# One decoder step: x loaded and turned ahead of the modulation, query rows spread through device memory

## The reference

```python
mod = (silu(c) @ ada_w + ada_b)                      # c: 1 + 8 rows; ada_w: 1024 x 6144
sh1, sc1, g1, sh2, sc2, g2 = split(mod, 6)
h = rms_norm(x, norm1_w) * (1 + sc1) + sh1
proj = h @ w_in                                      # pooling, attention q k v, delta rule, gates
q_a, k_a = rms_norm(q_a), rms_norm(k_a)              # per head of 64
y = concat(pool_mixer, moba_attention, gated_delta_rule)
x = x + g1 * (y @ w_out)
h2 = rms_norm(x, norm2_w) * (1 + sc2) + sh2
x = x + g2 * ((silu(h2 @ w_gate) * (h2 @ w_up)) @ w_down)
```

## Time and profile before

| what | value |
|---|---|
| median of 3 runs | 603.79 us (603.11 to 609.97) |
| the profiled execution: its time, its span | 604.71 us, 603.0 us |
| mean granted TensorE clock | 0.952 of full |
| PE busy, PEld busy | 541.0 us (90%), 445.9 us (74%) |
| DVE, ACT, POOL busy | 347.3 us (58%), 168.2 us (28%), 44.2 us (7%) |
| DMA | 114.68 MB, mean 190 GB/s |

### The profile page before, as it was taken

The page is one execution under the profiler, slowest core; times in us unless marked ns, Lnnn a source line. Parts: engine busy times, 40 slices in busy tenths (PEclk is TensorE's granted clock), DMA queues, the critical chain, the costliest instruction groups (busy, mean ns, idle before and its releaser), DMA issues.

```text
span 603.0 us, 10197 instructions
## 1 busy us (share of the span) xinstructions
PE 541.0 (90%) x3917; PEld 445.9 (74%) x3917; DVE 347.3 (58%) x541; ACT 168.2 (28%) x235; POOL 44.2 (7%) x107
## 2 busy tenths in 40 slices
PE   4759999998899898988879789987999999999997
PEld 2428678576578776667554139876999999999996
DVE  1046276658688897956655536475565466454441
ACT  2310110632122223321000215253433434334331
POOL 7300000000102910000011000000000000000000
PEclk9888989989689999999989889997999999999999
DMA  5997338356129485725639998594546645545201
GB/s 196 304 344 241 91 120 279 117 127 221 60 70 302 140 264 167 253 78 203 208 90 386 365 359 290 161 289 156 181 152 198 197 153 191 171 162 192 72 20 37
DMA packets 99437, 114.68 MB, mean 190 GB/s; under 512 B 7343, under 2 KB 82240, under 8 KB 99372
## 3 DMA queue, kind: packets, MB, share of 16 engines
q1 hardware_dynamic: 93368, 104.46, 54.2%
q10 hardware_dynamic: 5188, 7.67, 3.8%
q0 software_dynamic: 832, 1.89, 0.8%
HBM read 111.20 MB, written 2.97 MB: 189 GB/s over the span
## 4 chain that ended last, share of the span: by engine, by line
PE 69%; DVE 16%; DMA 6%; ACT 4%; issue 3%; ACTq 1%; SPq 1%; DVEq 0%
PE bank L335 65%; DVE prod L917 3%; DVE s_all L1013 3%; DMA ring<-in_ada_w_dram 2%; DVE mats L917 2%; DMA ring<-in_w_out_dram 2%; DMA ring<-in_cache_v_dram 1%; DVE cv L1121 1%; DVE BTP L917 1%; PE bank L387 1%; PE bank L358 1%; ACT w_part L1704 1%; DMA prod<-in_dn_norm_w_dram 1%; ACT adaS L1536 1%; PE bank L518 1%
## 5 line engine op out<-in xcount | busy, mean ns | idle before, releaser
L335 PE MATMUL bank<-a_hi,w_part 128*128 128x264 f32 x832 | 154.5, 287 | 2.1 <-DVE a_lo L1458 2.1
L917 DVE TENSOR_TENSOR w_part<-ring,w_part 128x2048 fp32r<-128x2048 f32 (+1 forms) x38 | 84.9, 2236 | 90.8 <-ACT w_part L1704 90.8
L335 PEld LDWEIGHTS bank<-a_hi,w_part 128*128 128x128 f32 x832 | 130.8, 191 | 2.6 <-issue 2.6
L335 PE MATMUL bank<-a_lo,w_part 128*128 128x264 f32 x416 | 119.0, 286 | 0.0
L1704 ACT ACTIVATE w_part<-ring 128x2048 fp32r<-128x2048 f32 (+1 forms) x38 | 70.9, 1869 | 86.8 <-PE bank L335 75.4
L335 PE MATMUL bank<-hT,ring 128*128 128x264 f32 x352 | 87.4, 411 | 4.1 <-ACT proj L1559 2.1
L335 PEld LDWEIGHTS bank<-hT,ring 128*128 128x128 f32 x352 | 71.0, 204 | 20.2 <-issue 7.4
L335 PEld LDWEIGHTS bank<-a_lo,w_part 128*128 128x128 f32 x416 | 79.6, 191 | 0.1
L335 PE MATMUL bank<-hid_hi,w_part 128*128 128x264 f32 x352 | 64.9, 285 | 0.0
L335 PEld LDWEIGHTS bank<-hid_hi,w_part 128*128 128x128 f32 x352 | 54.6, 188 | 0.1
L335 PE MATMUL bank<-hid_lo,w_part 128*128 128x264 f32 x176 | 49.7, 283 | 0.0
(11 more groups left out here) (321 smaller groups left out, 569.6 us busy)
## 6 DMA issues: line engine op xcount, KB each, us to landing
ring<-in_ada_w_dram SPq DMA_DIRECT2D x24, 1024.0 KB, 7.1
ring<-in_cache_k_dram SPq DMA_DIRECT2D x64, 256.0 KB, 3.6
ring<-in_w_in_dram SPq DMA_DIRECT2D x11, 1024.0 KB, 6.0
ring<-in_w_gate_dram SPq DMA_DIRECT2D x11, 1024.0 KB, 5.3
ring<-in_w_up_dram SPq DMA_DIRECT2D x11, 1024.0 KB, 5.3
ring<-in_cache_v_dram SPq DMA_DIRECT2D x40, 256.0 KB, 4.1
ring<-in_w_down_dram SPq DMA_DIRECT2D x8, 1024.0 KB, 5.3
ring<-in_cache_v_dram ACTq DMA_DIRECT2D x24, 256.0 KB, 4.8
```

The costliest lines, as they stand in the source:

```text
L335: return pe.matmul(out, lhsT, rhs, start=start, stop=stop, skip_group_check=True)
L917: return v.tensor_tensor(out, a, b_, op)
```

## The change

In the first stage:
- SP issues the two loads of c and then goes straight to the ring. The eleven small loads into `rows` go to ACT's queue behind the loads of x, the page table to POOL's; SP waits for the table only ahead of the first K item.
- ACT's nine later small loads go to POOL's queue, behind the masks; the count row is made ahead of the masks, and VectorE's work on it stands at the very start and behind the copies of x.
- TensorE begins with eight `keep_awake` matmuls, then turns x, then c, then the rows, then adds up the mean square (chunk by chunk), and only then begins with the modulation. All copies out of the turns are VectorE's, the squares are ACT's, one chunk at a time.
- Groups 0 and 1 are multiplied one behind the other (banks 2 and 3); each turn comes a group later than its multiplication, and there are more `keep_awake` matmuls between. The first four chunks of `hT` are scaled when group 2 is reduced, the others when group 3 is.

In the attention of the decoding sequences `QB` is dropped from TensorE and ACT. POOL stores the eight query rows to a buffer in device memory and reads each row back with a transfer that writes it to all 128 partitions; the transfers of queries 2 to 7 wait until the half of `qb` is free and stand at chosen places of POOL's order.

```diff
@@ tensor
+            pe.wait_ge(sem("ident_made"), 1)
+            keep_awake(7, 8)
+            pe.wait_ge(sem("x_in"), 16 * (TT + 1))
+            for c in range(DC):
+                b = opened(f"xT{c}", 4 + c % 4)
...
+            pe.wait_ge(sem("c_silu"), 1)
+            b = opened("cT", 0)
...
+            pe.wait_ge(sem("rows_in"), 16 * 11)
+            b = opened("rowsT", 1)
...
+            b = opened("ss1", 6)
+            for c in range(DC):
+                pe.wait_ge(sem("sq1"), c + 1)
+                last = mm(b[:, 0:NT], ones[:, :], hT[:, c, :], c == 0, c == DC - 1)
+            closed(last, "ss1")
             pe.wait_ge(sem("cT_made"), 1)
-            for j in range(2 * D // IW // 2):
-                ada(j)
-                ada_turn(j)
-                if j == 1:
-                    square_sums("ss1", "sq1", hT)
+            ada(0, 2)
+            ada(1, 3)
+            ada_turn(0, 0)
+            ada(2, 2)
+            ada_turn(1, 1)
+            keep_awake(0, 4)
+            ada(3, 3, 2)
+            ada_turn(2, 0)
+            keep_awake(1, 3)
+            ada_turn(3, 1)
+            keep_awake(0, 8)
@@ vector
+            def norm_half(c0, c1):
+                modulation(1, R_N1, c0, c1)
+                norm_rows(0, c0, c1)
+                for c in range(c0, c1):
+                    inc(v.tensor_scalar(hT[:, c, 0:T], hT[:, c, 0:T], scA[:, c, 0:1], modT[:, c, 0:1], ALU.mult, ALU.add),
+                        "h1")
+            mod_reduce(0)
+            mod_reduce(1)
+            mod_reduce(2)
+            norm_half(0, DC // 2)
+            mod_reduce(3)
+            norm_half(DC // 2, DC)
@@ k_item
-                v.wait_ge(sem("qb"), q + 1)
+                v.wait_ge(sem(f"qb{q % 2}"), 16 * (q // 2 + 1))
@@ gpsimd
+            def spread_query(q):
+                if q >= 2:
+                    g.wait_ge(sem("k_scored"), q - 1)
+                g.dma_start(qb[:, q % 2, :], q_dram[q, :].partition_broadcast(P)).then_inc(sem(f"qb{q % 2}"), 16)
+            g.wait_ge(sem("q_rows8"), 1)
+            g.dma_start(q_dram[:, :], nat8[:, 0, :]).then_inc(sem("q_stored"), 16)
+            g.wait_ge(sem("q_stored"), 16)
+            for q in range(4):
+                spread_query(q)
             g.wait_ge(sem("ebc"), 1)
...
+            spread_query(4)
             g.wait_ge(sem("k_rows"), 2)
...
+            spread_query(5)
             g.wait_ge(sem("proj_out"), out_count(PCH - 1))
...
+            spread_query(6)
             g.wait_ge(sem("tails"), 3)
...
+            spread_query(7)
             g.wait_ge(sem("max_diag"), 1)
@@ sync
             cols = {"ada": ada_w, "win": w_in, "wout": w_out, "gate": w_gate, "up": w_up}
-            sp.wait_ge(sem("table_in"), 16)
             for it in stream:
                 kind, i = it
+                if it == ("k", (0, 0)):
+                    sp.wait_ge(sem("table_in"), 16)
```

More of the change, by code:

```diff
@@ L228, in build @@
         hidden = sb("hidden_f", [P, 2, NT])
+        q_dram = nc.dram_tensor("q_rows_dram", [NS, AW], F32, kind="Internal").ap()
         bank = [ctx.enter_context(nc.psum_tensor(f"bank{i}", [P, 512], F32)) for i in range(8)]
@@ L342, in keep_awake, with ada @@
                     mm(bank[b][:, 0:P], ident[:, :], ident[:, :])
[L345 to L361, removed]
+            def ada(j, b_=3, awake=0):
                 opened(f"ada{j}", b_)
                 for n in range(2):
+                    keep_awake(1, awake)
                     last = ada_half(j, n)
@@ L441, in to_rows8 @@
                 closed(last, name)
[L443 to L447, removed]
             def kv_rows(name, c0, ready, n):
@@ L928, in _ @@
             step(v.memset(st4[:, :, :], 0.0))
-            b = full(v, "rowsT")
-            step(v.tensor_copy(constT[:, 0:NR], b[:, 0:NR]))
-            v.sem_inc(bank_free[2], 1)
+            v.wait_ge(sem("iota_made"), 1)
+            for c in range(PCH):
+                for g in range(2):
+                    r = slice(64 * g, 64 * g + 64)
+                    step(v.tensor_scalar(rcnt[r, c, :], rcnt[r, c, :], float(WINDOWS[2 * c + g]), None, ALU.min))
+            for c in range(DC):
+                b = full(v, f"xT{c}")
+                freed(v.tensor_copy(xT[:, c, :], b[:, 0:NT]), f"xT{c}")
             b = full(v, "cT")
             freed(v.tensor_copy(cT[:, :, 0:NC], b[:, 0:DC * NC].rearrange("p (c r) -> p c r", c=DC)), "cT")
-            v.wait_ge(bank_free[3], frees_at("cT"))
+            v.wait_ge(bank_free[0], frees_at("cT"))
             v.sem_inc(sem("cT_made"), 1)
-            for c in range(0, DC, 2):
-                b = full(v, f"xT{c}")
-                freed(v.tensor_copy(xT[:, c, :], b[:, 0:NT]), f"xT{c}")
+            b = full(v, "rowsT")
+            freed(v.tensor_copy(constT[:, 0:NR], b[:, 0:NR]), "rowsT")
+            v.wait_ge(bank_free[1], frees_at("rowsT"))
+            v.reciprocal(rcnt[:, :, :], rcnt[:, :, :]).then_inc(sem("rcnt_made"), 1)
+            v.wait_ge(sem("root1"), 1)
+            step(v.reciprocal(rbc[:, 0, :], rbc[:, 0, :]))
+            step(tt(hT[:, :, :], xT[:, :, :], bc(rbc[:, 0:1, :], [P, DC, NT]), ALU.mult))
             def mod_reduce(j):
@@ L950, in modulation @@
                                             op0=ALU.add, op1=ALU.mult))
[L952 to L973, removed]
+            def norm_rows(sh, c0=0, c1=DC):
+                step(tt(hT[:, c0:c1, T:NT], hT[:, c0:c1, T:NT], scA[:, c0:c1, 1:NC], ALU.mult))
+                step(tt(hT[:, c0:c1, T:NT], hT[:, c0:c1, T:NT], modT[:, sh * DC + c0:sh * DC + c1, 1:NC], ALU.add))
@@ L1511, in _ @@
             a.dma_start(x_nat[0:NS, TT, :], x_sample[:, 0, :]).then_inc(sem("x_in"), 16)
+            for r, src, m in ((R_ADAB, ada_b, 6 * DC), (R_N1, norm1_w, DC), (R_N2, norm2_w, DC), (R_PS, pool_scale, PCH)):
+                a.dma_start(rows[r:r + m, :], src.rearrange("o (m p) -> (o m) p", p=P)).then_inc(sem("rows_in"), 16)
+            a.dma_start(rows[R_CW:R_Q, :], conv_w[0].rearrange("i (c p) -> (i c) p", p=P)).then_inc(sem("rows_in"), 16)
+            for n, src in enumerate((q_norm_w, k_norm_w, dn_norm_w)):
+                for w in range(2):
+                    a.dma_start(rows[R_Q + n:R_Q + n + 1, 64 * w:64 * w + 64], src).then_inc(sem("rows_in"), 16)
             a.wait_ge(sem("c_in"), 32)
             inc(a.activation(c_nat, c_nat, ACT.Silu), "c_silu")
[L1514 to L1530, removed]
+            for c in range(DC):
+                a.wait_ge(bank_free[4 + c % 4], frees_at(f"xT{c}"))
+                inc(a.activation(hT[:, c, :], xT[:, c, :], ACT.Square), "sq1")
             def ada_rows(j):
@@ L1561, in proj_out @@
                     a.sem_inc(sem("proj_out"), 1)
[L1563 to L1569, removed]
             def take(name, dst, rows_, cols, done):
@@ L1797, in _ @@
             g.sem_inc(sem("ident_made"), 1)
+            cnt_i = prod[:, 0:T].bitcast(I32)
+            step(g.iota(cnt_i, pattern=[[1, T]], base=1, channel_multiplier=0))
+            for c in range(PCH):
+                step(g.tensor_copy(rcnt[:, c, :], cnt_i))
+            g.sem_inc(sem("iota_made"), 1)
+            g.dma_start(table[:, :], page_table.rearrange("q n -> (q n)").unsqueeze(0)).then_inc(sem("table_in"), 16)
             step(g.memset(blk[:, :], 0.0))
@@ L1839, in _ @@
             g.sem_inc(sem("masks_made"), 1)
[L1840 to L1844, removed]
+            g.dma_start(pbuf, state_pool[0].rearrange("q t c -> q (t c)")).then_inc(sem("pbuf_in"), 16)
+            g.dma_start(cst[:, :], state_conv[0].rearrange("q t c -> (q t) c")).then_inc(sem("cst_in"), 16)
+            g.dma_start(wba[:, :, :], w_in[0].rearrange("(k p) n -> p k n", p=P)[:, :, PJ * P:]).then_inc(sem("wba_in"), 16)
+            g.dma_start(gcol[:, 0:1], a_log.rearrange("o h -> h o")).then_inc(sem("gcol_in"), 16)
+            g.dma_start(gcol[:, 1:2], dt_bias.rearrange("o h -> h o")).then_inc(sem("gcol_in"), 16)
+            for n in range(2 * PCH):
+                g.dma_start(poolw[64 * (n % 2):64 * (n % 2) + 64, n // 2, :], pool_w[0, n]).then_inc(sem("poolw_in"), 16)
             outs = [0]
@@ L1929, in _ @@
             sp.dma_start(c_nat[1:NC, :], c_sample).then_inc(sem("c_in"), 16)
[L1930 to L1935, removed]
-            sp.dma_start(table[:, :], page_table.rearrange("q n -> (q n)").unsqueeze(0)).then_inc(sem("table_in"), 16)
             cols = {"ada": ada_w, "win": w_in, "wout": w_out, "gate": w_gate, "up": w_up}
-            sp.wait_ge(sem("table_in"), 16)
             for it in stream:
                 kind, i = it
+                if it == ("k", (0, 0)):
+                    sp.wait_ge(sem("table_in"), 16)
                 if kind in "kv":
```

27 lines of the change are left out of this document (13 added, 14 removed).

## The result

The changed kernel took 598.06 us (median of 4 runs, 596.88 to 601.32), the kernel before 605.5 us beside it: a ratio of 0.9861, 95% interval 0.9821 to 0.9901. Run again as a control in a later set it stood at 0.9895 (0.9844 to 0.9947). The profiled execution took 596.88 us, the fastest of its four, with a span of 594.9 against 603.0.

The account below looks back on a forecast made before the run. The first stage was taken as bound by transfers from 10 to 39 us, then by the chain from ada7. -3.7 - 1.4 + 2.3 - 1.0 = -3.8 took 604.71 to 600.9, the median to 600.0; range 593 to 607.

Parts of the forecast that it names:

- W1's start: End of the first stage: the first projection matmul starts at 41.3 us instead of 45.01, 3.7 us gained.
- ada0's read: First stage: TensorE first reads ada0 at 21.6 us, before at 16.39; ada5 needs its slot, so the queue runs dry 1.6 us.
- the tail: First stage, from ada7's landing to W1's start: 5.1 us, 5.6 before.
- The clock of W1 and W2: First projections: added matmuls fill the stretch before W1 and raise the granted clock; gain 0 to 2.2 us, 1.4 taken.
- The query path: Query rows through device memory: K0 starts 8.2 us after the rows instead of 2.0; 2.3 us lost, up to 5.9.
- the slack of 5.9: Query rows to K0: K0 may start up to 2.0 + 3.9 = 5.9 us after the rows before anything follows.
- QB4: Removed TensorE spread at 175.40 us, where VectorE waits for TensorE: 1.0 us gained.
- the other spreads: Other query spreads: removing TensorE's gains nothing, as VectorE sets the pace; the transfers replacing them lose nothing.
- (a): Rival, first stage: the queue never runs dry, ada7 lands at 33.6, W1 starts at 38.7; -7.2, 596.6 us; chance 0.22.
- (b): Rival, first stage: x and the rows come late beside the weights, W1 starts at 43.5; -1.6, 602.2 us; chance 0.18.
- (c): Rival, query path: the spread reads one row 128 times and is served slowly; 616.2 us at 15 us; chance 0.10.

Follow-up runs that it names:

- front_only: The changed first stage with the old query path (TensorE spreads each row, ScalarE copies it), against the kernel before: 602.73 us, 0.9937.
- spread_only: The kernel before with only the query rows spread by reads from device memory: 607.29 us, 1.0005 against the kernel before.
- q0_by_pe: The changed kernel with query 0 alone spread by TensorE and copied by ScalarE: 599.13 us, 0.9893 against the kernel before.
- best: Changed kernel with small loads held until ada7 landed, 12 awake pairs ahead of x, group 2's turn between group 3's halves, query 0 by TensorE: 594.99 us, 0.9815.

## Why the prediction was right, and where it wasn't

The forecast of 600.0 was right in sign, and its range holds the result, but the gain was about twice as large. For the profiled execution it had -3.8 us, and -8.1 came. By its own terms:

- **W1's start** (-3.7): -3.2 in the first profile (45.01 to 41.79), -1.4 in the control's (43.57). The mechanism held: five slots, ada0's late read, a standstill at 20 to 23 us, the small loads on ada7. Sizes were off both ways. ada0's read was put at 21.6, one time, where it moves with the gap before x's turns: group 0 started at 18.8 in one execution and 21.7 in another. ada7 landed at 34.7 (36.2 forecast), and the tail took 7.0 us instead of 5.1, as the small loads had left TensorE idle and slow; in the control it was the other way round, ada7 at 38.8 and a tail of 4.7.
- **The clock of W1 and W2** (-1.4, bound 2.2): -2.5, 16.95 to 14.41 us. The added matmuls hold it: without them the same passes took 16.17.
- **The query path** (+2.3): +0.66, from the rows to W4's start 43.81 before and 44.47 after. The 16 KB store took 2.24 us, not 4.0, and the read 3.46, not 3.8; K0 came 6.44 after the rows, not 8.2, against the slack of 5.9. The Trainium skill, "DMA: Bandwidth & Descriptors", section "Anatomy of one DMA — SWDGE (gpsimd) path", by which the store was estimated at 2.04 and the read at 2.6, was near for the first and low for the second; its sum (-6.1, which makes 597.7; the prediction wrote near 597) was nearer than mine. "SBUF — State Buffer", section "A bandwidth-pool intuition that's wrong (but worth ruling out)", by which 11.7 us was the estimate for one row behind one port, did not show: 3.46.
- **QB4** (-1.0): -1.22. Right.
- **Not seen at all: W4** (-1.65). The prediction put the removal of the other spreads at nothing, because they "stand where VectorE sets the pace". That step failed: in K0 to K2 TensorE set the pace (the 3.89 us before `cext`), since QB0 and QB1 kept it behind the query rows ahead of W8. W4's passes in before, front_only, changed and spread_only, in this order:

```profile
121.75 9.00 PE L335 MATMUL bank<-hT,ring 128*128 128x264 f32 x32 [2.06 <-ACT proj L1559]
119.92 9.04 PE L336 MATMUL bank<-hT,ring 128*128 128x264 f32 x32 [2.05 <-ACT proj L1561]
116.94 7.36 PE L336 MATMUL bank<-hT,ring 128*128 128x264 f32 x32 [0.77 <-ACT proj L1555]
122.08 7.36 PE L336 MATMUL bank<-hT,ring 128*128 128x264 f32 x32 [0.27 <-ACT proj L1554]
```

The 14 profiles on record fall into two groups here. In all of them W4 starts 22.95 to 23.10 us after the convolution, whether TensorE is early or late. In the four kernels with a spread on TensorE ahead of W8 (before, front_only, q0_by_pe, best) VectorE waits for TensorE at CEXT (2.59 to 5.38 us), W10 runs in 7.39 us, and TensorE then stands idle for 2.05 to 3.10 us ahead of W4, whose passes take 9.00 to 9.05 us (granted clock 0.81). In the ten others TensorE waits at CEXT (4.62 to 7.07 us) and it is W10 that runs slowly (9.13 to 10.36 us); the idle time ahead of W4 is 0.27 to 1.36 us, and W4 takes 7.36 at 1.00. So the idle time, and the slow passes behind it, moved from W4 to W10, where they are hidden behind the convolution. front_only and spread_only switch this in either direction, with either first stage.

Summed from the first profile: -5.75 at W2's end, +0.28 to the rows, +0.66, -1.65, -1.22 make -7.7 of -8.1; the rest is spread over the later stages. That this closes so well is in part luck of the execution: in the control's profile, the slowest of its six executions, the same sum is -5.2 (172.85 against 178.01), and of that only -0.8 is left in the whole span. Of the rivals, (a) came nearest in time, 596.6, for another reason: the queue did run dry. (b)'s rows were not late (turned at 13.6), and (c)'s slow read did not come.

What stays open: what makes the end times of one kernel differ by 5 us, the later stages above all, and so how much of the whole's 1.0 to 1.4% each half carries. W1 without the last awake pairs but with the small loads late was not tried.

## What to carry to other kernels

An early start of a ring is worth only what the first read of its first slot lets through: find that read, and what stands before it on its engine. An idle gap that moves takes the slow passes behind it along: look whether they land on the chain or beside it. Work taken off an in-order engine is to be priced by the wait that goes with it, not by its busy time: a spread of 1 us kept 16 us of projection behind the query rows. The small loads cut the full queue here from ScalarE's queue as from GpSimd's, so place such loads where the next transfer has slack.

## What the hardware showed unexpectedly

- TensorE's first passes ran at about half speed, and the column of the granted clock doesn't show it. The 16 awake passes at 1.91 us took 3.78 us in every profile that has just these (0.24 each; 16 took 1.95 later). The column reads 1.00 there because the trace has no record of the clock yet: its first record, at 1.00, comes at 5.2 to 6.4 us in seven profiles and at 17.6 to 21.3 us in the other seven (before 19.3, control 20.3), and up to it the passes are slow. Where TensorE idled 2.18 us or more behind the awake passes (4 profiles), all chunks of x took 0.82 us and the first record is one of the late ones. Where it idled 1.04 or less (4 profiles) they took 0.52. At 1.29 to 1.79 (3 profiles) they began at 0.52 and went to 0.82 between 9 and 10 us, and there the column does read 0.50.
- 128 reads of one 2 KB row of device memory took 3.46 us for 256 KB the first time and 3.5 to 6.1 in the later ones (median 4.3), within what the stores of 256 KB on the same queue took (3.8 and 7.4 in the earlier trace rows). VectorE waited for the first alone.
- The small loads, with the two copies of state 0.46 MB, cut the ring when issued by GpSimd as they did from ScalarE: 109 to 148 GB/s in their worst 2 us in six profiles, 83 before (28 to 30 us; 73 in the first of the two). The Trainium skill, "DMA: Bandwidth & Descriptors", section "Issuing engines are not separate DMA queues", states that the transfers of all issuing engines run on the same 16 DMA engines and interleave; the traces agree.
